# HGRN2 stage of a hybrid decoder trunk: the diagonals of the own scores move from VectorE to ScalarE, and at head 2 two steps change places with weight splits

## The reference

```python
def hgrn2_mixer(x, w_in, w_o, g_norm, lower_bound):
    q, fz, i, g = jnp.split(x @ w_in, 4, axis=-1)
    q = jax.nn.silu(q)
    f = lower_bound + (1.0 - lower_bound) * jax.nn.sigmoid(fz)
    log_f = jnp.log(f)
    k = 1.0 - f
    o = hgrn2_chunk_scan(heads(q), heads(k), heads(i), heads(log_f))   # 8 heads of 128
    o = rms_norm(o, g_norm) * jax.nn.silu(g)
    return o @ w_o

# within a chunk: scores[t, s] = sum_k q[t, k] * k[s, k] * exp(b[t, k] - b[s, k]) for s <= t
```

## Time and profile before

| | |
|---|---|
| time, 3 runs | 968.34 us median (968.09 to 968.36) |
| profiled execution | 967.88 us |
| its span in the profile | 966.1 us |
| TensorE matmul busy | 956.1 us, 99% |
| VectorE busy | 848.8 us, 88% |
| ScalarE busy | 564.8 us, 58% |
| GpSimd busy | 37.9 us, 4% |
| stage C | about 640 to 768 us of the span |

### The profile page before, as it was taken

How to read it: one execution, slowest core, us unless ns; L and a number is a source line. 1 busy time by engine, 2 the same in 40 slices (tenths; PEclk the granted TensorE clock), 3 DMA queues, 4 the chain that set the end, 5 groups by cost and what they waited for, 6 DMA issues and landing times.

```text
span 966.1 us, 12770 instructions
## 1 busy us (share of the span) xinstructions
PE 956.1 (99%) x4520; PEld 792.9 (82%) x4520; DVE 848.8 (88%) x1208; ACT 564.8 (58%) x627; POOL 37.9 (4%) x64
## 2 busy tenths in 40 slices
PE   9999999999999999999999999999999999999996
PEld 7888888888888888888888888888888888888885
DVE  5999888996888999899899998999898998888896
ACT  6665556436645555565565555549898545565650
POOL 0100000000210000000000000000100100000000
PEclk9999999999999999999999999999999999999999
DMA  9686566553657565665566565735233655565631
GB/s 305 221 267 239 195 199 222 190 181 125 225 196 237 179 213 179 213 217 174 177 216 216 174 218 179 257 113 192 88 132 121 228 196 193 180 215 176 214 133 43
DMA packets 129312, 184.47 MB, mean 191 GB/s; under 512 B 5968, under 2 KB 104800, under 8 KB 129136
## 3 DMA queue, kind: packets, MB, share of 16 engines
q1 hardware_dynamic: 126032, 173.56, 54.5%
q0 software_dynamic: 2672, 9.77, 2.8%
q10 hardware_dynamic: 560, 0.52, 0.2%
HBM read 182.78 MB, written 1.05 MB: 190 GB/s over the span
## 4 chain that ended last, share of the span: by engine, by line
PE 95%; DVE 3%; ACT 1%; issue 0%; DMA 0%; POOL 0%; DVEq 0%; ACTq 0%
PE psum L1711 29%; PE psum L1720 29%; PE psum L1715 29%; PE psum L1886 2%; PE psum L2235 1%; PE psum L1704 1%; PE psum L2221 1%; DVE w_lo L937 0%; DMA raw<-in_ffn_w_in 0%; ACT w_hi L482 0%; PE psum L1970 0%; PE psum L1990 0%; PE psum L2207 0%; DVE w_lo L967 0%; PE psum L2039 0%
## 5 line engine op out<-in xcount | busy, mean ns | idle before, releaser
L937 DVE TENSOR_TENSOR w_lo<-raw,w_hi 128x2048 fp32r<-128x2048 f32 x125 | 284.8, 2282 | 7.5 <-ACT w_hi L482 7.3
L1711 PE MATMUL psum<-w_hi,xT 128*128 128x512 f32 x959 | 266.1, 394 | 0.6 <-DVE arena L1469 0.4
L1720 PE MATMUL psum<-w_hi,xT 128*128 128x512 f32 x959 | 261.7, 390 | 0.2 <-DVE xT L1011 0.2
L1715 PE MATMUL psum<-w_lo,xT 128*128 128x512 f32 x959 | 261.5, 389 | 0.0
L482 ACT CAST w_hi<-raw 128x2048 fp32r<-128x2048 f32 x125 | 238.7, 1916 | 23.0 <-DMA raw<-in_ffn_w_in 16.1
L1720 PEld LDWEIGHTS psum<-w_hi,xT 128*128 128x128 f32 x959 | 180.1, 188 | 38.5 <-DVE xT L1011 0.5
L1715 PEld LDWEIGHTS psum<-w_lo,xT 128*128 128x128 f32 x959 | 180.0, 188 | 37.6
L1711 PEld LDWEIGHTS psum<-w_hi,xT 128*128 128x128 f32 x959 | 176.8, 188 | 37.4 <-DVE ffn_tok L1069 1.3
L519 ACT ACTIVATE ffn_tok<-psum 128x256 f32<-128x256 f32 x88 | 33.8, 384 | 204.3 <-PE psum L1715 195.4
L1711 PE MATMUL psum<-w_hi,hT_hi 128*128 128x512 f32 x316 | 99.5, 403 | 0.0
L1715 PE MATMUL psum<-w_lo,hT_hi 128*128 128x512 f32 x316 | 95.6, 391 | 0.0
(11 more groups left out here) (202 smaller groups left out, 817.9 us busy)
## 6 DMA issues: line engine op xcount, KB each, us to landing
raw<-in_ffn_w_in SPq DMA_DIRECT2D x170, 512.0 KB, 4.8
raw<-in_ffn_w_out SPq DMA_DIRECT2D x88, 512.0 KB, 4.0
raw<-in_c_w_in SPq DMA_DIRECT2D x32, 512.0 KB, 4.5
raw<-in_ab_w_in SPq DMA_DIRECT2D x16, 512.0 KB, 4.8
raw<-in_ab_w_o SPq DMA_DIRECT2D x8, 512.0 KB, 3.7
raw<-in_c_w_o SPq DMA_DIRECT2D x8, 512.0 KB, 3.7
ln_gb<-in_ln_gain POOLq DMA_DIRECT2D x6, 512.0 KB, 6.4
ln_gb<-in_ln_bias POOLq DMA_DIRECT2D x6, 512.0 KB, 7.2
```

Source lines behind the costliest of these rows:

```text
L937: nc.vector.tensor_tensor(w_lo[:, slot_of[n]], raw[:, n % RAW], w_hi[:, slot_of[n]].bitcast(F32), ALU.subtract).then_inc(lo_ready, 1)
L1711: nc.tensor.matmul(dst, a_hi, b_hi, start=first, stop=False)
L1715: ins = nc.tensor.matmul(dst, a_hi, b_lo, start=False, stop=final and last)
L1720: ins = nc.tensor.matmul(dst, a_lo, b_hi, start=False, stop=final and last)
```

## The change

`head_own` is taken from VectorE's list and a function of that name is put into ScalarE's, once for each head right after `head_squares` of the head before (for head 0 after `head_kqT(0)`). It makes the same two diagonals with an activation (Copy, scale read from `kq_own`). Two semaphores tie it: `own_sums` from `decays`, and `own_ready`, for which `upper_scores` now waits. At head 2, VectorE does `queries(2, 0)` ahead of `split(7)`, where it was behind it, and ScalarE does `head_cross(2)` ahead of `split(8)`. TensorE's, GpSimd's and SyncE's lists are as they were.

```diff
@@ scalar engine, mix_c
                 head_kqT(0)
+                head_own(0)
                 split(3)
...
                 head_squares(0)
+                head_own(1)
                 log_decay(1)
...
                 sigmoids(2, 0, G[0])
                 head_squares(1)
+                head_own(2)
                 sigmoids(2, 1, G[1])
                 head_norm(1)
+                head_cross(2)
                 split(8)
-                head_cross(2)
                 split(9)
                 head_exp(3, 0)
                 head_exp(3, 1)
                 head_squares(2)
+                head_own(3)
                 head_kqT(4)
...
+            def head_own(hd):
+
+                act.wait_ge(S["own_sums"], 2 * (hd // 2) + 2)
+                if hd:
+                    act.wait_ge(S["head_done"], hd)
+                for t in range(TT):
+                    own = kq_own[:, (hd // 2) % 2, t, hd % 2:hd % 2 + 1]
+                    ins = nc.scalar.activation(scT[:, t], ident[:], ACT.Copy, scale=own)
+                ins.then_inc(S["own_ready"], 1)
@@ vector engine, mix_c
                 logf_split(1)
-                own = head_own(2)
                 split(6)
                 upper_factors(2)
                 lower_factors(2)
+                queries(2, 0, G[0])
                 split(7)
-                queries(2, 0, G[0])
-                lower_scores(2, upper_scores(2, own))
+                lower_scores(2, upper_scores(2))
...
                 lower_factors(6)
-                own = head_own(6)
                 split(12)
-                lower_scores(6, upper_scores(6, own))
+                lower_scores(6, upper_scores(6))
...
-            def head_own(hd):
-
-                if hd:
-                    dve.wait_ge(S["head_done"], hd)
-                for t in range(TT):
-                    own = kq_own[:, (hd // 2) % 2, t, hd % 2:hd % 2 + 1]
-                    ins = nc.vector.tensor_scalar(scT[:, t], ident[:], own, None, ALU.mult)
-                steps[0] += 1
-                ins.then_inc(dve_step, 1)
-                return steps[0]
...
-            def upper_scores(hd, written):
+            def upper_scores(hd):
 
                 dve.wait_ge(S["levels_done"], 2 * hd + 1)
+                dve.wait_ge(S["own_ready"], hd + 1)
```

More of the change, by code:

```diff
@@ L777, in mix_c @@
                 head_squares(3)
+                head_own(4)
                 head_norm(3)
@@ L786, in mix_c @@
                 head_squares(4)
+                head_own(5)
                 log_decay(3)
@@ L794, in mix_c @@
                 head_squares(5)
+                head_own(6)
                 head_norm(5)
@@ L803, in mix_c @@
                 head_squares(6)
+                head_own(7)
                 gates(1, 0, G[0])
@@ L1388, in mix_c @@
                 logf_split(0)
-                own = head_own(0)
                 split(3)
@@ L1393, in mix_c @@
                 split(4)
-                lower_scores(0, upper_scores(0, own))
+                lower_scores(0, upper_scores(0))
                 split(5)
                 queries(1, 0, G[0])
-                own = head_own(1)
                 decays(1, 0)
@@ L1402, in mix_c @@
                 decays(1, 1)
-                lower_scores(1, upper_scores(1, own))
+                lower_scores(1, upper_scores(1))
                 logf_split(1)
-                own = head_own(2)
                 split(6)
@@ L1416, in mix_c @@
                 lower_factors(3)
-                own = head_own(3)
                 split(8)
-                lower_scores(3, upper_scores(3, own))
+                lower_scores(3, upper_scores(3))
                 logf_split(2)
-                own = head_own(4)
                 split(9)
@@ L1425, in mix_c @@
                 split(10)
-                lower_scores(4, upper_scores(4, own))
+                lower_scores(4, upper_scores(4))
                 queries(3, 0, G[0])
                 decays(3, 0)
-                own = head_own(5)
                 upper_factors(5)
@@ L1433, in mix_c @@
                 decays(3, 1)
-                lower_scores(5, upper_scores(5, own))
+                lower_scores(5, upper_scores(5))
                 logf_split(3)
@@ L1438, in mix_c @@
                 lower_factors(6)
-                own = head_own(6)
                 split(12)
-                lower_scores(6, upper_scores(6, own))
+                lower_scores(6, upper_scores(6))
                 head_gate(0, 0, 0, 2)
                 head_gate(0, 1, 0, 2)
-                own = head_own(7)
                 split(13)
@@ L1450, in mix_c @@
                 split(14)
-                lower_scores(7, upper_scores(7, own))
+                lower_scores(7, upper_scores(7))
                 oT_split(0)
@@ L1485, in decays @@
                         op0=ALU.mult, op1=ALU.add, accum_out=kq_own[:, g % 2, t, h:h + 1])
-                step(ins)
+                ins.then_inc(S["own_sums"], 1)
+                dve.wait_ge(S["own_sums"], 2 * g + t + 1)
             def logf_split(g):
@@ L1540, in lower_factors @@
                 ins.then_inc(S["factors_ready"], 1)
-            def head_own(hd):
-                if hd:
-                    dve.wait_ge(S["head_done"], hd)
-                for t in range(TT):
-                    own = kq_own[:, (hd // 2) % 2, t, hd % 2:hd % 2 + 1]
-                    ins = nc.vector.tensor_scalar(scT[:, t], ident[:], own, None, ALU.mult)
-                steps[0] += 1
-                ins.then_inc(dve_step, 1)
-                return steps[0]
             def level_copy(n, written):
                 one = "p (n t j) -> p n t j"
-                dve.wait_ge(dve_step, written)
+                if written is not None:
+                    dve.wait_ge(dve_step, written)
                 ins = nc.vector.copy_predicated(query_places(LEVELS[n]),
```

2 lines of the change are left out of this document (added).

## The result

| | before | after |
|---|---|---|
| time, 9 runs each | 968.09 us median (967.39 to 968.37) | 970.57 us median (970.13 to 971.70) |
| ratio | | 1.0027, 95% interval 1.0018 to 1.0036 |
| profiled execution, its span | 967.88, 966.1 us | 971.70, 969.9 us |
| VectorE, ScalarE busy | 848.8, 564.8 us | 846.2, 568.9 us |

The change makes the kernel 2.5 us slower by the medians, 1.7 to 3.5 us by the interval. 970.57 lies 0.2 us under the forecast of 970.8 and inside its range.

The account below looks back on a forecast made before the run. TensorE bounds the kernel, matmuls filling 956.1 of 966.1 us; ScalarE is full in two stretches of stage C. 1.06 + 1.45 = +2.5 us on 967.88 gives 970.4, plus 0.46 for the median: 970.8 us, range 967.8 to 971.6.

Parts of the forecast that it names:

- The likeliest case: Stage C: VectorE's weight splits hold GpSimd at head 2 and head 6; 970.2 to 971.5 us, chance 0.48.
- The two prices: A diagonal pair takes 0.51 us of ScalarE; GpSimd's step on SBUF waits for the end of VectorE's running weight split.
- Heads 0 and 1: Early diagonals delay `split(3)`'s copies and reload, then ScalarE: 0 to 0.45 us, taken as +0.36 at head 3's transposes.
- what it waits for moves too: At 664.64 ScalarE's 0.45 us wait for a load doesn't absorb the delay, since that load is later too.
- Head 2: `queries(2, 0)` first ends a 0.6 us wait, but `split(7)` holds GpSimd later: norm of head 1 0.6 us later.
- Head 3: Cross copy 1.49 us later, TensorE waits before head 5's transposes; less 0.43 for `logf_split`, net +1.06 us.
- Head 6 and 7: `split(12)` starts sooner and holds GpSimd; norm of head 5 +1.83 us, TensorE's outputs of head 7 +1.45 us.
- the tie: Head 6: `split(12)` starts at 736.25, GpSimd's first step 0.02 us behind; only its second step was taken as held.
- the case in brackets: Head 6: norm 2.0 to 2.1 us later if GpSimd's whole second step or both steps come after the split.
- Rival 1: GpSimd isn't held at head 6, or has slack behind; only +1.06 or +0.7 remains: 969.0 to 969.5 us, chance 0.26.
- Rival 2 and 3: 2: ScalarE's head 3 chain isn't the limit, 967.4 to 968.6 us, 0.16; 3: all is won, 966.4 or less, 0.03.
- Rival 4: Both GpSimd steps held, a pair at 0.62 us, a load late: +0.25 + 0.3 + 0.3, 971.7 us and over, chance 0.07.

Follow-up runs that it names:

- own3_twice: Kernel before with head 3's diagonals alone on ScalarE, made there twice, the second pair to memory nobody reads; 968.57 us against 968.17.
- own2_twice: Kernel before with head 2's diagonals alone on ScalarE, made there twice, the second pair to memory nobody reads; 968.25 us against 968.17.
- own_only: The changed kernel with both moves of head 2 undone, all eight pairs of diagonals still on ScalarE; 970.37 us against 968.09 before.
- own6_alone: Kernel before with only the pair of diagonals of head 6 moved to ScalarE; 969.87 us against 968.09.
- split12_late: The changed kernel with VectorE's weight split of head 6, `split(12)`, moved behind that head's lower scores; 968.99 us against 968.09 before.
- order_only: The changed kernel with all diagonals back on VectorE, both moves of head 2 kept; 968.31 us against 968.09 before.
- split7_late: order_only with VectorE's `split(7)` moved behind the decays of head 2's second query tile; 967.75 us against 968.17 before.
- split7_late_own: split7_late with all eight pairs of diagonals on ScalarE and `split(12)` behind head 6's lower scores; 967.85 us against 968.17 before.

## Why the prediction was right

The likeliest case happened in each of its parts. That the sum came so close is in part luck: three terms were mis-sized, by -0.20, +0.09 and +0.24 us, and for the most part cancel (+2.51 forecast, +2.63 measured in the stage, +2.48 by the medians). The 0.2 us between 970.8 and 970.57 come from none of them: I had added the change to a median of 968.34 us from three runs of the kernel before, and nine give 968.09.

- **The two prices.** The pair on ScalarE takes 0.60 us in a full stretch (655.58 to 656.18 of after, and four activations 0.29 us apart above), not 0.51:

```profile
655.58 0.69 ACT L896 ACTIVATE arena<-ident,kq_own 128x128 f32<-128x128 f32 x2
656.18 1.89 ACT L484 CAST w_hi<-raw 128x2048 fp32r<-128x2048 f32 x1
```

  The row that I took it from reads PSUM. By the Trainium skill ("ScalarE: Activation LUTs", What ACT_TABLE_LOAD costs) the estimate was 0.59; the trace agrees with it, and it should have had more weight than a row of another source. GpSimd is held to the end of the split, as taken: +0.05 us at both places of after. A power with 0.57 us left behind the split, which I took for head 6, didn't occur there; where a power was held elsewhere it ended 0.55 us after what held it (last section).
- **Heads 0 and 1**, forecast +0.36, came to +0.16. The step that failed is "what it waits for moves too". ScalarE is 0.58 us late ahead of the load for which it waited 0.45 us, and 0.11 us late behind it (664.64 before; 665.94 less 1.19 after), with no wait left:

```profile
665.94 1.91 ACT L484 CAST w_hi<-raw 128x2048 fp32r<-128x2048 f32 x1
```

  The load was sent off 0.5 us later, but it took 5.1 us in place of 5.5 (4.5 to 5.5 us over all these traces). At `log_decay(1)` 0.17 us are left, which is also what VectorE is late there: 0.58 us from `split(3)`, for which it now waits for ScalarE, less the 0.39 of its own diagonals of head 1. All four kernels with the early pairs on ScalarE show the same 0.16 or 0.17 us at the outputs of head 1.
- **Head 2**, norm and all behind it +0.6: measured 0.6.
- **Head 3**, cross copy forecast 1.49 us later: 707.34 against 704.80, less 1.19 of offset, is +1.35 (0.16 + 0.60 + 0.60). TensorE's net +1.06: measured +1.00 by its steps, +0.91 with the small ones. That it would lose 0.69 of it already at the levels wasn't foreseen as a place; the sum doesn't change by it. own3_twice and own2_twice show that ScalarE has no gap here and has one a head earlier.
- **Head 6 and 7**, forecast +1.45: measured +1.69 by its steps, and 1.72 with the small ones, as in own_only and own6_alone. The step mis-sized is the tie. I let GpSimd's first step win it and the second be held, norm +1.83; in after the split was 0.02 us ahead, the first step was held for the whole split, and the norm came 7.51 us behind the exponentials of head 6 (733.98 to 741.49) where it was 5.42 (731.89 to 737.31): +2.09, the case in brackets. VectorE's start at head 7 then moved by 1.75 and not 1.48.
- **The rivals.** Rival 1 (no hold at head 6) is what split12_late makes by hand: 968.99 us, the low end of its price of 969.0 to 969.5. Rival 2 and 3 need spare time of ScalarE between 690 and 705 us, of which there is none. Rival 4 came true in two of its parts, the full hold of head 6 and the dearer pair, but its third, a late load, didn't.

By the Trainium skill ("SBUF — State Buffer", Who interferes with whom) a VectorE instruction with two SBUF inputs and a GpSimd one that reads SBUF share a read port, and the first to issue keeps it. The one half agrees here: GpSimd is held for 1.45 to 2.62 us behind a running split, and free (0.19 and 0.74 us) where the split began after the step. The other half doesn't show: a split that starts 0.11 us into a running power takes its usual 2.28 us (736.58 of order_only), where by the rule it would wait, and this is so in every kernel here that has this order. The measurement decides: in these runs only GpSimd's instruction gets long. That it is the port and not something else that the two engines share, no run here separates.

## What to carry to other kernels

Taking work off an engine lets its next instruction start sooner; ask what that one shuts out. Here a long VectorE instruction with two SBUF sources, started 0.4 us sooner, shut out a 0.2 us step of GpSimd on which a full ScalarE hung. A wait of the bounding engine is won only if the engine that is full behind it gets no later: find the stretch without gaps and count what enters it. And when the hold is removed, look at once for what stands just behind it; on top of the reordering it took four moves on two engines to keep 1.4 us in the traces, where the first alone kept 0.24.

## What the runs showed of the hardware that I had not expected

- Hundredths decide who waits. A split 0.01 to 0.03 us ahead of the small step held it for 2.31 or 2.32 us, in three kernels of three. The power shows both sides. At the norm of head 4 it started 0.03 us ahead of a multiply of `decays` with both inputs in SBUF (L1498) and took its 0.70 us; in split7_late it started 0.05 us behind and took 0.93. Rows of order_only, then of split7_late:

```profile
723.97 0.70 POOL L1712 TENSOR_TENSOR ssq<-ssq,mhalf 128x2 f32<-128x2 f32 x1
724.00 0.44 DVE L1498 TENSOR_TENSOR arena<-arena,ln_gb 128x256 f32<-128x256 f32 x1
```

```profile
723.26 0.43 DVE L1498 TENSOR_TENSOR arena<-arena,ln_gb 128x256 f32<-128x256 f32 x1
723.31 0.93 POOL L1712 TENSOR_TENSOR ssq<-ssq,mhalf 128x2 f32<-128x2 f32 x1
```

- So the second GpSimd step, the power, is held in the same way, behind a split for 2.62 us where it takes 0.70 (756.95 of split7_late_own). It ended 0.55 us after that split, and 0.55 us after the multiply above, so most of its own work came after; the small step ends 0.05 us after what held it. If the split starts while the power runs, 0.11 us in, the power takes 0.74 us and the split its usual 2.28.
- Activations of 128 columns with a scale read from SBUF, in a row, start 0.29 us apart though each is shown 0.39 us long.
